# Gathering the experts' rows by rank, during or after the last expert steps of a two-layer encoder trunk

## The reference, cut to what matters

```python
h = rmsnorm(x, norm_ffn_g[l]) * (1.0 + sc2) + sh2
y = swiglu(h2, w_shared_gu[l], w_shared_down[l]) + moe_routed(
    h2, router_w[l], router_bias[l], w_exp_gu[l], w_exp_down[l])
x = x + g2 * y.reshape(b, s, d)
```

## Time and profile before

| | |
|---|---|
| median of 3 runs | 3136.98 us (3135.05 to 3143.74) |
| profiled execution, its own time | 3136.87 us |
| its span | 3135.2 us |
| TensorE busy | 2880.7 us (92%) |
| VectorE busy | 2031.5 us (65%) |
| ScalarE busy | 1586.0 us (51%) |
| GpSimd busy | 646.8 us (21%) |
| mean granted TensorE clock | 0.959 of full |

### The profile page before, as it was taken

The page is one execution under the profiler, slowest core; times in us unless marked ns, Lnnn a source line. Parts: engine busy times, 40 slices in busy tenths (PEclk is TensorE's granted clock), DMA queues, the critical chain, the costliest instruction groups (busy, mean ns, idle before and its releaser), DMA issues. The chain is left out here.

```text
span 3135.2 us, 42239 instructions
## 1 busy us (share of the span) xinstructions
PE 2880.7 (92%) x13740; PEld 2189.2 (70%) x13740; DVE 2031.5 (65%) x2871; ACT 1586.0 (51%) x2482; POOL 646.8 (21%) x563
## 2 busy tenths in 40 slices
PE   5999998899899999999589999989998999999994
PEld 4677775677577777777466777756776777777773
DVE  4544445554588888888645444465546888888884
ACT  2342423432357777777334334244333777777771
POOL 1000000100034653333010000000001356433330
PEclk9999999999899999999779999999998999999995
DMA  7123332233569999999512243313334999999975
GB/s 226 63 88 141 107 140 75 90 110 131 199 250 360 362 366 370 359 361 362 206 58 76 89 139 113 135 61 106 119 110 185 354 358 349 368 367 366 362 272 215
DMA packets 119884, 671.46 MB, mean 214 GB/s; under 512 B 27565, under 2 KB 28973, under 8 KB 84237
## 3 DMA queue, kind: packets, MB, share of 16 engines
q1 hardware_dynamic: 86368, 605.91, 51.9%
q0 software_dynamic: 31424, 57.44, 5.5%
q10 hardware_dynamic: 1932, 6.16, 0.8%
HBM read 656.60 MB, written 55.28 MB: 227 GB/s over the span
## 5 line engine op out<-in xcount | busy, mean ns | idle before, releaser
L1981 DVE TENSOR_TENSOR ew_lo<-ew,e_hi 128x2048 fp32r<-128x2048 f32 x258 | 591.6, 2293 | 184.6 <-ACT e_hi L1783 184.6
L706 PE MATMUL bank<-h_hi,w_hi 128*128 128x512 f32 x1248 | 514.9, 413 | 57.1 <-DVE w_lo L640 22.2
L1783 ACT ACTIVATE e_hi<-ew 128x2048 fp32r<-128x2048 f32 x260 | 497.4, 1914 | 79.2 <-PE bank L2179 79.2
L640 DVE TENSOR_TENSOR w_lo<-raw,w_hi 128x1024 fp32r<-128x1024 f32 x198 | 242.5, 1225 | 418.3 <-ACT w_hi L632 417.8
L706 PE MATMUL bank<-h_hi,w_lo 128*128 128x512 f32 x1248 | 505.4, 405 | 0.0
L706 PE MATMUL bank<-h_lo,w_hi 128*128 128x512 f32 x1248 | 503.5, 403 | 0.0
L2179 PE MATMUL bank<-e_hi,x_hi 128*128 128x512 f32 x1040 | 418.2, 402 | 0.1
L2179 PE MATMUL bank<-ew_lo,x_hi 128*128 128x512 f32 x1040 | 407.5, 392 | 0.0
L2179 PE MATMUL bank<-e_hi,x_lo 128*128 128x512 f32 x1040 | 405.4, 390 | 0.0
L632 ACT ACTIVATE w_hi<-raw 128x1024 fp32r<-128x1024 f32 x198 | 208.3, 1052 | 285.9 <-DMA raw<-in_wmix 172.4
L706 PEld LDWEIGHTS bank<-h_hi,w_hi 128*128 128x128 f32 x1248 | 241.6, 194 | 145.1 <-issue 50.9
(11 more groups left out here) (319 smaller groups left out, 4436.1 us busy)
## 6 DMA issues: line engine op xcount, KB each, us to landing
ew<-in_wexp SPq DMA_DIRECT2D x130, 2048.0 KB, 9.7
raw<-in_wmix SPq DMA_DIRECT2D x297, 512.0 KB, 4.0
ew<-in_wexp SPq DMA_DIRECT2D x130, 1024.0 KB, 9.8
yt<-y_d SPq DMA_DIRECT2D x4, 3072.0 KB, 19.7
yt<-y_d SPq DMA_DIRECT2D x4, 2048.0 KB, 10.6
ada0a<-in_ada SPq DMA_DIRECT2D x2, 2048.0 KB, 13.4
ada0b<-in_ada SPq DMA_DIRECT2D x2, 2048.0 KB, 22.2
h_d<-htok ACTq DMA_DIRECT2D x8, 512.0 KB, 11.9
```

The lines of the kernel that those rows point to most:

```text
L640: nc.vector.tensor_tensor(w_lo[q % SPLIT][:], raw[u % RAW][:], w_hi[q % SPLIT][:].bitcast(F32), ALU.subtract).then_inc(lo_done, 1)
L706: ins = nc.tensor.matmul(out, lhs, rhs, start=start, stop=stop)
L1783: nc.scalar.activation(e_hi[h][:], up_part(ew, j, h), ACT.Copy).then_inc(whi_done, 1)
L1981: nc.vector.tensor_tensor(up_part(ew_lo, j, h), up_part(ew, j, h), e_hi[h][:].bitcast(F32), ALU.subtract).then_inc(wlo_done, 1)
```

## The change

1. The six rows of a token in `y_d` are ordered by the number of the expert. VectorE compares the six chosen numbers pairwise and counts how many are smaller; that count is the rank, and row 8 * token + rank takes the result. This stands after the indices have become floats (after L1905).
2. The overflow block goes from position 64 to position 61 (`OV = NE - 3`). Experts 61, 62 and 63 go to positions 62, 63 and 64. Rank 0 can then only belong to an expert up to 58, rank 3 to one up to 61, rank 5 to one up to 63.
3. Rows are loaded rank by rank (512 tokens, 2 MB, rows of 4 KB that lie 32 KB apart) into parts of the weight buffers, on SP, as soon as positions are scattered and the buffers are free: ranks 0 to 2 after position 61, rank 3 after 62, rank 4 after 63, rank 5 after 64. Rank 4 and 5 come in two halves of two token tiles each.
4. VectorE adds ranks instead of rows of a tile; the first half of rank 1 is added before the last copy of expert results.
5. The combining no longer has blocks of its own. Each engine goes on in the same block. Tiles alternate between the banks `G` and `SB`.
6. The sums of squares have a 128x128 of ones as weights and move the 128 columns of squares. Every partition then holds the sum of each token; four operations of VectorE pick the diagonal and make the mean.

```diff
+OV = NE - 3
+            y_rows = y_d.rearrange("(t p k) d -> p t k d", p=P, k=YROWS)
+            up_of = [ew[i][:, 0:KD * S].rearrange("p (t d) -> p t d", t=TC) for i in range(4)]
+            down_of = [ew[i][:, KD * S:].rearrange("p (t d) -> p t d", t=2) for i in range(4)]
+            ranks = [[up_of[i][:, 0:2], up_of[i][:, 2:4]] for i in (1, 2, 3, 0)] + [[down_of[1], down_of[2]], [down_of[3], down_of[0]]]
+            row_sum = up_of[1]
+            def wait_rows_landed(eng, e):
+                for s in range(4):
+                    eng.wait_ge(y_out[s], 16 * ((e - s) // 4 + 1))
+            def load_rank(sp, r, sems_of):
+                if r < 4:
+                    sp.dma_start(up_of[(1, 2, 3, 0)[r]], y_rows[:, :, r, :]).then_inc(sems_of[0], 16)
                 else:
+                    for h in range(2):
+                        sp.dma_start(ranks[r][h], y_rows[:, 2 * h:2 * h + 2, r, :]).then_inc(sems_of[h], 16)
...
+            def dve_combine_rows(dve):
...
+                link(dve, add_rank(1, 1))
+                dve.wait_ge(rank_in[1], 16)
+                link(dve, add_rank(2, 0))
+                link(dve, add_rank(2, 1))
+                dve.sem_inc(ysum, 1)
+                dve.wait_ge(rank_in[2], 16)
+                link(dve, add_rank(3, 0))
+                link(dve, add_rank(3, 1))
+                dve.wait_ge(rank_in[3], 32)
+                link(dve, add_rank(4, 0))
+                last_rank(0)
+                last_rank(1)
+                link(dve, add_rank(4, 1))
+                add_back(0)
+                last_rank(2)
+                add_back(1)
+                last_rank(3)
+                add_back(2)
...
+                dve.wait_ge(ysq_sum, TC - 1)
+                for t in range(TC):
+                    if t:
+                        dve.wait_ge(ymean, t)
+                    mean(t)
...
+            def pe_combine(pe):
...
+                            ins = nc.tensor.matmul((OB if t == TC - 1 else MB)[:, t * P:(t + 1) * P], ones[:], sqc[t % 2][:, k, :], start=k == 0,
+                                                   stop=k == KD - 1)
+                    ins.then_inc(ysq_sum, 1)
...
+                turn(0)
+                turn(1)
+                turn(2)
+                sums(0)
+                turn(3)
+                for t in range(1, TC):
+                    sums(t)
...
-                    load_down(over, 0)
+                    load_down(weights_of(NE), 0)
+
+                    wait_rows_landed(sp, NE - 3)
+                    sp.wait_ge(dn_ready, NE - 2)
+                    load_rank(sp, 0, rank_sems[0])
+                    sp.wait_ge(gu_used, 2 * NE - 2)
+                    load_rank(sp, 1, rank_sems[1])
+                    sp.wait_ge(gu_used, 2 * NE)
+                    load_rank(sp, 2, rank_sems[2])
+                    wait_rows_landed(sp, NE - 2)
+                    sp.wait_ge(gu_used, 2 * NE + 2)
+                    load_rank(sp, 3, rank_sems[3])
+                    wait_rows_landed(sp, NE - 1)
+                    sp.wait_ge(dn_ready, NE - 1)
+                    load_rank(sp, 4, rank_sems[4])
+                    wait_rows_landed(sp, NE)
+                    sp.wait_ge(dn_ready, NE + 1)
+                    load_rank(sp, 5, rank_sems[5])
...
+                    link(dve, nc.vector.tensor_tensor(less, topf[:, :, 0:TOPK].unsqueeze(3).broadcast_to(pairs),
+                                                      topf[:, :, 0:TOPK].unsqueeze(2).broadcast_to(pairs), ALU.is_gt))
+                    link(dve, nc.vector.tensor_reduce(destf[:].rearrange("p (t a) -> p t a", t=TC), less, AX.X, ALU.add))
+                    link(dve, nc.vector.scalar_tensor_tensor(yrow[:], yrow[:], float(YROWS), destf[:], ALU.mult, ALU.add))
...
                     turned(NE, 8)
+                    dve.wait_ge(rank_in[0], 32)
+                    link(dve, add_rank(1, 0))
+                    dve.sem_inc(ysum, 1)
                     y_half(dve, NE // 8 - 1, 8)
```

More of the change, by code:

```diff
@@ L323, in hybrid_trunk @@
         yrow = place("yrow", [P, NPAIR])
+        pick = place("pick", [P, P])
         cursor[0] = keep_end
@@ L1536, in down_part, with sp_combine, pool_combine @@
                 return w[j % 4][:, KD * S:].rearrange("p (f c) -> p f c", f=2)
+            tile_bank = (G, SB)
+            def sp_combine(sp):
+                sp.wait_ge(ysum, 2)
+                sp.dma_start(vec[:], vec_d[1 - l, :, 0:NVEC]).then_inc(pre_in, 16)
+                for u in range(RAW):
+                    sp.dma_start(raw[u][:], wmix_d[(1 - l) * NTILES + u]).then_inc(pre_in, 16)
+                sp.wait_ge(pre_in, 16 + 16 * RAW)
+            def pool_combine(pool):
+                pool.wait_ge(ymean, TC)
+                nc.gpsimd.tensor_tensor(rstd[:, 0:TC], stat[:, 0:TC], mhalf[:, 0:TC], ALU.pow)
@@ new lines, in dve_combine_rows, with last_rank, add_back, mean @@
+            def dve_combine_rows(dve):
+                def last_rank(t):
+                    if t % 2 == 0:
+                        dve.wait_ge((rank_in[4], over_in)[t // 2], 16 * (t // 2 + 1))
+                    v = row_sum[:, t, :]
+                    nc.vector.tensor_tensor(v, v, ranks[TOPK - 1][t // 2][:, t % 2, :], ALU.add).then_inc(ysum, 1)
+                def add_back(t):
+                    dve.wait_ge(yscaled, 2 * t + 2)
+                    x = xT[:, :, t * P:(t + 1) * P]
+                    nc.vector.tensor_tensor(x, x, sc[t % 2][:], ALU.add).then_inc(yadd, 1)
+                def mean(t):
+                    dve.wait_ge(ysq_sum, t + 1)
+                    own = (OB if t == TC - 1 else MB)[:, t * P:(t + 1) * P]
+                    nc.vector.tensor_tensor_reduce(out=pick[:], in0=own, in1=ident, scale=1.0 / D, scalar=EPS, op0=ALU.mult,
+                                                   op1=ALU.add, accum_out=stat[:, t:t + 1]).then_inc(ymean, 1)
+                link(dve, add_rank(1, 1))
[16 more added lines that the diff above has]
+                add_back(2)
+                for b in range(2):
+                    dve.wait_ge(ytr, 2 * (TC - 1) + b + 1)
+                    for k in range(4):
+                        x = xT[:, 4 * b + k, (TC - 1) * P:]
+                        ins = nc.vector.scalar_tensor_tensor(x, tile_bank[(TC - 1) % 2][b][:, k * P:(k + 1) * P],
+                                                             mod[:, 40 + 4 * b + k:41 + 4 * b + k], x, ALU.mult, ALU.add)
+                    ins.then_inc(yadd, 1)
+                dve.wait_ge(ysq_sum, TC - 1)
[3 more added lines that the diff above has]
+                    mean(t)
@@ L1600, in _ @@
                                          ).then_inc(o_load, 16)
-                    sp.wait_ge(y_done, 1)
-                    for t in range(3):
-                        load_rows(sp, t)
+                        sp.wait_ge(o_turn, nb)
+                        sp.wait_ge(ysum, 1)
+                        for r in range(TOPK):
+                            load_rank(sp, r, rank_sems[r])
+                    sp_combine(sp)
                 @block.gpsimd
@@ L1704, in _ @@
                     scatter(NE // 8 - 1, 7)
[L1705 to L1711, removed]
+                    scatter(NE // 8 - 1, 8)
                     nb = blocks(pool)
@@ L1730, in _ @@
                             pool.sem_inc(o_turn, 1)
-                    for s in range(4):
-                        pool.wait_ge(y_out[s], 16 * (NE // 4 + (s == 0)))
-                    pool.sem_inc(y_done, 1)
+                    pool_combine(pool)
                 @block.scalar
```

207 lines of the change are left out of this document (80 added, 127 removed).

## The result

The changed kernel is faster. On the first chip it took 3108.5 us (median of 4, 3101.6 to 3112.57), the kernel before 3140.36 us (median of 4): a ratio of 0.9893, with a 95% interval of 0.9875 to 0.9911, or 28 to 39 us. Run again as the control of the experiments it stood at 0.9918 (0.9897 to 0.9940). The forecast of 3104 us, 33 us less, lies in the first interval and outside the second, which ends at 32.

The account below looks back on a forecast made before the run. It took late loading of 12.58 MB of y, then VectorE's adds and TensorE's half-clock sums, as the bound after the experts. 16.7 less 0.2 gave 16.5 us a layer, 33 in two: 3136.9 to 3104 us, range 3092 to 3118.

Parts of the forecast that it names:

- From a scatter's start to SP's issue: Wait before a rank's load: 3.2 us when the queues are empty, 6.1 us in the loaded expert stage.
- Rival 3: Rank loads in strided 4 KB pieces run slowly, at 200 GB/s losing 10 us a layer: 3157 us; chance 0.05.
- rival 4: Half the gain: loads at 300 to 360 GB/s, branch of 5 or 6 us, or no load-move overlap: 3116; chance 0.10.
- The last y copy: VectorE's add ahead of it ends before TensorE's last result, so costs nothing; cover 1.1 us.
- The six adds: VectorE, rank 1's second half to rank 4's first: 13.9 us from 1526.6 to 1540.5, bounded by VectorE, not transfers.
- the branch: VectorE's new count read and branch after the last y copy, put at 1.5 us, between about nothing and 6.2.
- If the rise comes late in tile 1's sums: TensorE's clock rises during the sums, tiles 2 and 3 take half: sums end about 1561.7, taken as 1562.
- bring nothing: By the skill page, tile 2's and 3's transposes do not help raise TensorE's clock; only the sums count.
- Rival 1: TensorE's clock stays at 1.2 GHz; sums end at 1565.1, 13.4 us a layer gained: 3110 us; chance 0.20.
- Rival 2: TensorE's clock is up at once; sums end about 1557.5, 21 us a layer gained: 3095 us; chance 0.12.
- Two block boundaries go; both lay beside the wait for rows, so nothing: Removing the combining's block boundaries was put at no gain and no cost.
- rival 5: More than one overflow block, so all six ranks are loaded again; chance 0.01.

Follow-up runs that it names:

- e0: The changed kernel unchanged, run again as the control; ratio to the kernel before 0.9918 (0.9897 to 0.9940).
- e1: The changed kernel with one GpSimd drain added after its last scatter, before it waits for the means; ratio to the kernel before 0.9877.
- e6: The kernel before with only the ordering of a token's rows by expert number added; ratio to the kernel before 1.0002 (0.9990 to 1.0014).
- e8: The changed kernel with a GpSimd drain added ahead of the last two scatters; one execution, 3092.74 us, no interval.
- e2: The changed kernel with sums of squares as before (squares as weights, one column of ones moved); ratio to the kernel before 0.9944.
- e4: The changed kernel with the first half of rank 1 added after the last y copy instead of ahead; ratio to the kernel before 0.9924.

## Why the prediction was right, and what in it was not

**The transfers.** The path was right, and the times nearly to the microsecond. Ranks 0 to 2 were to be issued about 1507.5 and were from 1507.16; rank 3 was to follow at 1520.4 and did at 1520.33; rank 5 at 1532.8, measured 1531.50. Only rank 4 came later (1529.49 against 1527.6): its scatter started at 1522.10 and took 2.22 us beside the busy VectorE. The terms under these times were less good than the times. From a scatter's start to SP's issue I had 3.2 us and three times 6.1; it took 3.2, 6.0, 7.4 and 4.2. In rank 5's case two errors partly cancel: its scatter started 0.6 us late and then took 1.9 us less to land than I had put. The GB/s line of the changed kernel over 1505 to 1545 us, in 40 equal slices, shows the strided 4 KB pieces at some 410 from 1510 on, with one dip between 1529 and 1532:

```profile
GB/s 115 45 0 188 274 434 410 422 410 422 422 406 414 410 410 410 410 422 393 410 401 414 406 414 332 160 258 385 393 430 414 426 414 406 418 414 395 411 410 410
```

Rival 3, slow pieces, needed less than 242 GB/s, and rival 4 rates of 300 to 360, a branch of 3.5 us or more (VectorE's idle time there is 0.65) or no overlap of load and move (tile 0's sums in layer 2 take 3.62 us at the lower clock, about what one-column sums take, and not twice that). Both fall. The last y copy, whose cover I put at 1.1 us, was not delayed: VectorE idled 1.26 us before it.

**VectorE.** The six adds were to run from 1526.6 to 1540.5 and ran from 1526.14 to 1540.18; the branch that I put at 1.5 us left 0.65 of idle time. The last tile's sum was due at 1550.0 and came at 1549.7. In layer 2 VectorE waited 0.44 and 0.25 us for ranks 4 and 5, so the transfers are close behind it as a bound.

**The clock, a mis-sized term.** "If the rise comes late in tile 1's sums" gave 1562 for the end of the sums; they ended at 1558.26. The term had the rise too late: in both layers it came ahead of tile 1's sums, in tile 3's transposes, and the three tiles' sums ran wholly at 2.4 GHz, 1.84 us each. The changed kernel's windows of one microsecond, four of layer 1 and three of layer 2:

```profile
1544.00:1545.00 1.00, 1.00 (x7) 0.94 (x5) 0.89 (x1) 1.00 (x5) 0.00 (x0) 0.50 1.03 410
1545.00:1546.00 1.00, 0.35 (x2) 0.00 (x0) 0.90 (x1) 1.00 (x5) 0.00 (x0) 0.89 0.56 209
...
1548.00:1549.00 1.00, 1.00 (x10) 1.00 (x9) 1.00 (x2) 0.80 (x5) 0.00 (x0) 0.81 0.00 0
...
1552.00:1553.00 1.00, 1.00 (x11) 1.00 (x10) 0.49 (x2) 1.00 (x1) 0.00 (x0) 0.98 0.00 0
...
3083.00:3084.00 1.00, 1.00 (x6) 1.00 (x6) 0.23 (x1) 0.00 (x0) 0.00 (x0) 0.50 0.00 0
3084.00:3085.00 1.00, 1.00 (x9) 1.00 (x8) 0.14 (x1) 0.88 (x1) 0.00 (x0) 0.69 0.00 0
3085.00:3086.00 1.00, 1.00 (x12) 1.00 (x11) 1.00 (x5) 0.18 (x1) 0.00 (x0) 1.00 0.00 0
```

In layer 1, after 16 transposes and no product, the clock is up from about 1545.2; after the idle time that follows it falls in 1548 to 1549, and is up again by 1552. The Trainium skill ("TensorE: Matmul & The Clock Gate", Part 4) says that transposes don't count as busy in this way. In layer 1 the measurement differs, and it decides. So the sentence that by that page transposes "bring nothing" failed in layer 1, though the early rise was worth little: 0.9 us on tile 2's transposes, before it was lost. In layer 2 the same 16 transposes brought no rise (the clock stays at 0.50 to 3084). That such a rise is not certain shows in the other runs as well: the eight transposes of tile 2 took 1.1 us in some layers and 1.97 in others, in the same kernel (e0: 1.10 in both layers; changed: 1.10 and 1.97). Tile 0's sums take between 1.95 and 3.6 us accordingly. Rival 1, a low clock to the end, falls. Rival 2, up at once, had the sums end 21 us a layer earlier; they did by 20.8 and 18.5, so for the clock it was nearer than the forecast, and its 3095 was missed mainly by the drain.

**The block boundary, wrong.** The step is "Two block boundaries go; both lay beside the wait for rows, so nothing", with "what follows (the mean, GpSimd's power, the barrier) is kept". That the boundary lay beside the wait was true, and that was the point: what lies beside a wait is paid there. GpSimd's 6.6 us of drain moved to the end of the layer. It had been put at nothing and measured 6.6 us a layer; e1 shows that it is worth 12.5 us in the stretches and 12.9 in the medians. I had read for GpSimd only rows of work; its drain of 6.6 us stood in the trace of before as well, under the line of the block.

**The sum.** Per layer 16.5 us was forecast. In layer 1 the sums end 20.8 us earlier, less 0.2 for the mean and 6.6 for the drain: 14.0. In layer 2 18.5 us, with the same losses: 11.7. Two errors of opposite sign, +4 and +2 against -6.6 twice, left 25.7 against 33. The medians' own scatter (28 to 39 us in the first set, 19 to 32 in the second) reaches from there to the forecast. So the hit at 3104 is in part luck: the clock term, put too low, and the drain, left out, pull in opposite directions.

**The rest.** The ordering costs nothing that the time shows (e6: at most 0.0014, 4 us). More than one overflow block, rival 5, did not occur.

## What to carry to other kernels

When blocks of instructions are merged or a barrier is dropped, list what each engine does at the boundary, the drains too, and ask where that goes: work that was free beside a wait can land on the path, and one line that did it early got it back here (e1). Look at the wait before you place that line: in e8, among the last scatters, the drain held the rows back. When a load is moved under compute, first look for the stretch in which the transfer engines are idle, then take the waits of each buffer and each scatter in order; that sum came out within 2 us here. For short TensorE work after an idle stretch, prefer the form that moves columns to the one that loads weights for a single column, at the same number of instructions.

## What the runs showed of the hardware that I had not expected

- GpSimd's drain takes 6.6 us after the experts' block with its 154 indirect transfers (7.7 with the power of 1.05 in it), 1.16 with the power after an earlier drain, and 1.32 after two more scatters. After the mixer's block, with 40 plain transfers and no indirect one, it takes 4.4 with a power of 1.03 in it.
- 16 transposes of 128x128 after 17 us of idle time brought TensorE's clock from 1.2 to 2.4 GHz in some layers and not in others. 10.2 us of one-column products, back to back, never did (before, e2, e6); with 128 columns moved the last 48 entries ran at 2.4 GHz in every layer of the changed kernel and took 5.5 to 5.6 us.
- Rows of 4 KB that lie 32 KB apart come at about 410 GB/s, little under the 428 of 16 to 24 KB pieces.
- A scatter's instruction on GpSimd takes 2.2 us beside VectorE's add of 128x2048 and 0.90 with that add moved away and nothing else changed (e4, both layers).
